# A decoder layer in float32: 16 of the weight sums of each down projection formed in the rounds before it

## The chip, the cores and the metric

The kernel runs on one core of a Trainium2 chip (trn2). The metric is the time of one execution on the device, in microseconds (us). The core has TensorE (PE, matmuls), VectorE (DVE), ScalarE (ACT), GpSimd (POOL) and SyncE (SP), which issues all the transfers between HBM and the on-chip memory; its queue is SPq in the rows.

## The reference, cut to what matters

```python
for i in range(DEPTH):                                  # DEPTH = 1, SEQ = 1024, D_MODEL = 1024, D_FF = 2816
    h = swiglu(rmsnorm(x, ffn1_pre_norm[i]), ffn1_w_gate[i], ffn1_w_up[i], ffn1_w_down[i])
    x = x + MACARON_WEIGHT * rmsnorm(h, ffn1_post_norm[i])
    h = hybrid_mixer(rmsnorm(x, mix_pre_norm[i]), ...)
    x = x + rmsnorm(h, mix_post_norm[i])
    h = swiglu(rmsnorm(x, ffn2_pre_norm[i]), ffn2_w_gate[i], ffn2_w_up[i], ffn2_w_down[i])
    x = x + MACARON_WEIGHT * rmsnorm(h, ffn2_post_norm[i])

def swiglu(x, w_gate, w_up, w_down):
    return (jax.nn.silu(x @ w_gate) * (x @ w_up)) @ w_down
```

The change touches the two feed-forward blocks (`f1` and `f2`) alone.

## The kernel before

**Precision and form.** Every float32 product is made of three matmuls in a faster format, from a high and a low part of each operand: hi x hi, hi x lo, lo x hi. ScalarE makes the high part (a cast), VectorE the low one (a subtraction). Large products are formed as seven smaller ones in place of eight, after Strassen's scheme; some of their operands are sums or differences of two blocks, which VectorE has to form first.

**The rounds.** A feed-forward block has 22 tiles of 128 hidden features. The first two are made plainly, the others in pairs: the loop variable `i` goes from 1 to 10, and each pair has the tiles `s = 0` and `s = 1`. `seven_pe` gives PE's order for one tile: seven products of 12 matmuls of 512 columns. `tile` in `ffn_dve` gives VectorE's: it takes the products out of PSUM, scales them, multiplies the up half by the gated half into `act_stage`, and in between forms the sums and low parts (`t3_sum`, `t2_sum`, `v1_low`, `t3_low` and so on) of the next tile. Where it does this differs by `s`: in tile `s = 0` `t3_sum` and `t2_sum` stand right after the third product's reads (L983, L985), ahead of the sum of L999; in tile `s = 1` they stand after L999 and L1001. PE's seventh product waits for L999 (`read(4)`), the first product of the next tile for `v1_low` (L895). SP loads the next tile's weights: `g_next` (gate, 512 KB, L410) waits until all seven low parts of the tile are formed, since the last of them, `g2_low` (L922), still reads the gate buffer; `v_next` (up, two loads of 256 KB, L413) waits for PE's products 1 and 4; `store` writes a tile's activations to HBM (L432). All of them stand in one queue in this order:

```python
                    g_next(i, 0)
                    v_next(i, 0, 0)
                    store(i - 1, 1)
                    v_next(i, 0, 1)
                    g_next(i, 1)
                    v_next(i, 1, 0)
                    store(i, 0)
                    v_next(i, 1, 1)
```

Before round 8 SP also issues the three loads of the first rows of activations for the down phase, 5.5 MB (`down_first_rows_sp`, L1308).

**The down phase** multiplies by the down weights: seven products `m = 0` to 6, each over `k = 0` to 10, four output parts `d`, 12 matmuls for a step `(m, k)`. The weight block of a step is a single block of the input (`m` = 2, 5) or a sum or difference of two: `DOWN_W` lists them. For these SP loads two blocks of 256 KB (`down_w_in`), VectorE adds them (`down_w_sum`, L1357), ScalarE casts (`down_w_hi`, L1372) and VectorE forms the low part (`down_w_lo`, L1388). The activations go the same way (`down_b_sum` L1363, `down_b_hi` L1383, `down_b_lo` L1395). Steps use 9 (f1) or 11 (f2) buffers in turn; the first ones are filled near the end of the rounds. The order of the down phase's steps on each engine isn't written by hand: `Plan.order` places them by costs and ranks given in `down_steps`, `first_turn_steps` and `end_plan`, together with what follows the block (the sums of squares, residuals and norms, and after f1 the first projections of the mixer).

Of the kernel before, what the change touches and what calls it, by code (L numbers as in the profile page):

```python
# [20 lines left out]
P = 128  # L21
# [59 lines left out]
    return (FG * m + k) % len(DOWN_SLOTS[p])  # L81


def w_loads(p, m, k):
    n = down_slot_of(p, m, k)
    return sum(min(len(DOWN_W[a]), 2) for a in range(m + 1) for b in range(FG)
               if (a, b) <= (m, k) and down_slot_of(p, a, b) == n)


W_SUMS = FG * sum(len(u) > 1 for u in DOWN_W)  # L90
B_SUMS = FG * sum(len(u) > 1 for u in DOWN_B)
FFN_COUNTS = {"gu_in0": 16, "gu_in1": 16, "gu_hi": PLAIN, "gu_lo": PLAIN, "gu_mm": 2 * PLAIN, "gate": 2 * PLAIN,
              "up": 2 * PLAIN, "silu": 2 * PLAIN, "prod": 2 * PLAIN, "s_act": 12, "s_dve": 21, "g_in": 16 * SEVEN,
# [3 lines left out]
              "dn_b_sum": B_SUMS, "dn_w_hi": FG * DOWN_N, "dn_b_hi": FG * DOWN_N, "dn_w_lo": FG * DOWN_N,  # L97
              "dn_b_lo": FG * DOWN_N, "dn_step": (FG - 1) * DOWN_N, "dn_mm": 4 * DOWN_N, "dn_put": len(PUTS),
              "dn_sum": len(SUMS), "dn_w_in9": 0, "dn_w_in10": 0}
for _n in range(9):  # L100
    FFN_COUNTS[f"dn_w_in{_n}"] = 16 * max(w_loads("f1", a, b) for a in range(DOWN_N) for b in range(FG)
                                          if down_slot_of("f1", a, b) == _n)
SHARED = {"dn_w_in0": ("turn_hi", KT), "dn_w_in1": ("turn_lo", KT), "dn_w_in2": ("turn_sq", KT), "dn_w_in3": ("turn_sum", KT - 1),
          "dn_w_in4": ("first_w_in", 16), "dn_w_in5": ("cols_in", 32), "dn_w_in6": ("consts_in", 64),
          "dn_w_in7": ("half_cols", 1), "dn_w_in8": ("first_w_hi", 1), "dn_b_first": ("first_w_lo", 1),
          "dn_b_second0": ("rope_sin", 2), "dn_w_in9": ("sd_x_mm", CH), "dn_w_in10": ("sd_cb_mm", CH)}
JOINT = {n: f"{old}_{new}" for new, (old, _) in SHARED.items() for n in (old, "ff_" + new)}


def build(nc, a):  # L110
    with ExitStack() as ctx:  # L111
        sems = {}

        def sem(name):
            if name[:3] in ("f1_", "f2_"):
                name = "ff_" + name[3:]
            name = JOINT.get(name, name)
            if name not in sems:
                sems[name] = ctx.enter_context(nc.semaphore(name))
            return sems[name]  # L120
# [6 lines left out]
        def wait(eng, name, value):  # L127

            if not isinstance(value, int) or value > 0:

                eng.wait_ge(sem(name), value + (FFN_COUNTS[name[3:]] if name[:3] == "f2_" else 0)
                            + (SHARED[name[3:]][1] if name[3:] in SHARED and name[0] == "f" else 0))


        nh = at("norm_hi", 0, [P, KT, S], FR)
# [121 lines left out]
        dsum = {p: at("down_sums_" + p, kb, [P, KT, S]) for p, kb in DOWN_SUMS.items()}  # L257
        res3 = at("residual_closing", 0, [P, KT, S])
        late = at("late_tokens", 64, [P, KT, S])
        dw_hi, dw_two, dw_lo, dw_raw, db_hi, db_lo, db_raw = ({} for _ in range(7))  # L260
        for p, slots in DOWN_SLOTS.items():
            dw_hi[p] = [at(f"{p}_down_w_hi_{n}", w, [P, 4, P], FR) for n, (w, _) in enumerate(slots)]
# [11 lines left out]


        acts = nc.dram_tensor("act_scratch", (FT, P, S), F32).ap()
        x1 = nc.dram_tensor("x1_scratch", (KT, P, S), F32).ap()
        x2 = nc.dram_tensor("x2_scratch", (KT, P, S), F32).ap()
        zscr = nc.dram_tensor("z_scratch", (Z_T, P, S), F32).ap()
# [141 lines left out]
        def ffn_sp(sp, p, wgu):  # L421
            def g_next(i, s):
                wait(sp, p + "_t_lo", at_tile(i, s, 7, 7))
                g_in_sp(sp, p, pair_of(wgu, i, s + 1))

            def v_next(i, s, n):
                wait(sp, p + "_seven", at_tile(i, s, 7, 4 if n else 1))
                v_in_sp(sp, p, pair_of(wgu, i, s + 1), n)

            def store(i, s):  # L430
                wait(sp, p + "_read", at_tile(i, s, 11, 11))
                sp.dma_start(pair_of(acts, i, s), stage[p][0][:]).then_inc(sem(p + "_act_out"), 16)  # L432
# [12 lines left out]
            def rounds(first, last):
                with sp.Fori(first, last) as i:
                    g_next(i, 0)
                    v_next(i, 0, 0)
                    store(i - 1, 1)
                    v_next(i, 0, 1)  # L450
                    g_next(i, 1)
                    v_next(i, 1, 0)
                    store(i, 0)
                    v_next(i, 1, 1)
            rounds(2, FIRST_ROWS)
            down_first_rows_sp(sp, p)
            rounds(FIRST_ROWS, LAST_PAIR)
            g_next(LAST_PAIR, 0)
            v_next(LAST_PAIR, 0, 0)
            store(LAST_PAIR - 1, 1)  # L460
            v_next(LAST_PAIR, 0, 1)
            down_start_sp(sp, p, store)


# [323 lines left out]
        def ffn_dve(v, p, t, pre):  # L788
# [181 lines left out]
                    else:  # L970
                        turn_half_dve(v, step, e, cols[:, 24:32], cols[:, pre:pre + KT])

            def tile(i, s, more):
                def product(n):
                    wait(v, p + "_seven", at_tile(i, s, 7, n))

# [22 lines left out]
                v.tensor_tensor(e4[:], banks(3), e4[:], ALU.add).then_inc(sem(p + "_read"), 1)  # L999
                had(4)  # L1000
                v.tensor_tensor(e4[:], e4[:], rb[:, half(0)], ALU.mult).then_inc(sem(p + "_read"), 1)  # L1001
                if s and more:
                    t3_sum(i, s + 1)
                    t2_sum(i, s + 1)
# [39 lines left out]
            tile(1, 0, True)  # L1044
            tile(1, 1, True)
            with v.Fori(2, LAST_PAIR) as i:
                tile(i, 0, True)
                tile(i, 1, True)
            tile(LAST_PAIR, 0, True)
            tile(LAST_PAIR, 1, False)  # L1050
            yield
# [12 lines left out]
        def down_steps(plan, p):  # L1064
# [8 lines left out]
            for m in range(DOWN_N):  # L1073
                for k in range(FG):
                    n = FG * m + k
                    ready = []
                    if n >= EARLY:
                        free = ("mm", *divmod(n - slots, FG)) if n >= slots else None
                        if n >= slots:
                            add("SP", "dw_in", ("dw_in", m, k), 6.0, free)  # L1080
                            if (m, k) == (1, 3):
                                add("SP", "dw_in", ("late_in",), 4.0)
                            elif (m, k) == (1, 6):
                                add("SP", "dw_in", ("b_in",), 4.0)
                        w = ("dw_in", m, k) if n >= slots else ("db_lo", m, k - 1) if k > EARLY else None
                        if len(DOWN_W[m]) > 1:
                            add("DVE", "w_sum", ("dw_sum", m, k), 0.61, w)
                            w = ("dw_sum", m, k)
                        add("ACT", "w", ("dw_hi", m, k), 0.54, w)
                        add("DVE", "w", ("dw_lo", m, k), 0.61, ("dw_hi", m, k))  # L1090
                        b = free
                        if len(DOWN_B[m]) > 1:
                            add("DVE", "b_sum", ("db_sum", m, k), 0.61, free)
                            b = ("db_sum", m, k)
                        add("ACT", "b", ("db_hi", m, k), 0.54, b)
                        add("DVE", "b", ("db_lo", m, k), 0.61, ("db_hi", m, k))
                        ready = [("dw_lo", m, k), ("db_lo", m, k)]
                    if k == 0 and m > 1:
                        ready += [u for d in range(4) for u in put_in(m - 2, d)]
                    if k == 0 and m == last:  # L1100
                        ready.append(end)
                    add("PE", "main", ("mm", m, k), 2.04 if p == "f2" and m == last else 2.72, *ready)
                if p == "f2" and m == last:
                    add("PE", "main", ("last",), 7.5)
                for d in range(4):
                    done = ("last",) if p == "f2" and (m, d) == (last, 3) else ("mm", m, FG - 1)
                    users = put_in(m, d)
                    for u in users:
                        engine = "ACT" if u[0] == "put" else "DVE"
                        before = [w for n in range(m) for w in put_in(n, d) if w[2:] == u[2:]]  # L1110
                        other = {(1, "add"): users[0], (4, "put"): users[-1]}.get((m, u[0]))
                        add(engine, u[0], u, 0.69, done, before[-1] if before else None, other)
# [140 lines left out]
        RSTD_RANK = {(x, "rstd"): 0 for x in ("PE", "ACT", "DVE")}  # L1253

        def w_sums(m, k):
            return FG * sum(len(x) > 1 for x in DOWN_W[:m]) + k + 1

        def b_sums(m, k):
            return FG * sum(len(x) > 1 for x in DOWN_B[:m]) + k + 1
# [39 lines left out]
        def down_w_in(sp, p, m, k):  # L1299
            down_slot(sp, p, m, k)  # L1300
            j = down_slot_of(p, m, k)
            for n, (out, rows) in enumerate(DOWN_W[m][:2]):
                to = dw_two[p][j] if n else dw_raw[p][j]
                sp.dma_start(to[:], a["d" + p[1]][FG * rows + k][:, 4 * out:4 * out + 4]).then_inc(sem(f"{p}_dn_w_in{j}"), 16)
# [60 lines left out]

        def down_w_hi(act, p, m, k):
            j = down_slot_of(p, m, k)
            if len(DOWN_W[m]) > 1:
                wait(act, p + "_dn_w_sum", w_sums(m, k))
            else:  # L1370
                down_w_loaded(act, p, m, k)
# [1912 lines left out]
```

## Time and profile before

| | us |
|---|---|
| median of 3 runs | 2229.76 (2228.91 to 2235.98) |
| the profiled execution, whole | 2235.22 |
| its span, first to last instruction | 2233.4 |
| PE busy | 2175.1 |
| DVE busy | 1748.0 |
| ACT busy | 1012.1 |

The mean granted clock of TensorE is 0.992. Rounds of block f1 run from about 65 to 450 us, its down phase to 666; the mixer to about 1560; rounds of f2 from about 1620 to 2000, its down phase to 2220. In a timeline row the first number is the start, the second the time of the instruction (or of x n of them in a row), and the brackets tell how long the engine was idle before it and what ended that.

### The profile page before, as it was taken

To read this page: it belongs to the slowest core of one execution; us is meant where nothing else is said; L and a number is where in the kernel's file an instruction comes from. 1 tells how busy PE (TensorE), PEld (TensorE's weight loads), DVE (VectorE), ACT (ScalarE), POOL (GpSimd) and SP (SyncE) were. 2 spreads that over 40 slices of the span, in tenths; PEclk is the share of its full clock that TensorE was granted. 3 is DMA by queue.
4 is the path that set the end of the run, shared out by engine and by line. 5 is a ranking of instruction groups with operands and counts; after the bars stand their busy time and mean duration, and the time that the engine had idled before them with its cause. 6 is when DMAs were issued, how large, how long until landed. Compare 5 with 4: busy or idle time off the path is not lost. (4 is left out here: it accounts for less than half of the span.)

```text
span 2233.4 us, 29464 instructions
## 1 busy us (share of the span) xinstructions
PE 2175.1 (97%) x10148; PEld 1778.8 (80%) x10148; DVE 1748.0 (78%) x2707; ACT 1012.1 (45%) x1837; POOL 229.5 (10%) x213
## 2 busy tenths in 40 slices
PE   9999999999998999999999999999999999999998
PEld 7788887878877877778788777788888888887887
DVE  8777777799898787786666676878877777779988
ACT  6323332255553576787632684323522322335454
POOL 0000000000000344444200233300000000000000
PEclk9999999999999999999999999999999999999999
DMA  4222234385453001001131124223132224247644
GB/s 145 66 85 85 85 119 154 95 310 176 164 192 102 29 10 38 31 18 58 42 102 48 64 107 172 83 79 120 66 95 85 83 83 170 83 154 269 224 139 160
DMA packets 101608, 245.00 MB, mean 110 GB/s; under 512 B 10752, under 2 KB 12800, under 8 KB 99968
## 3 DMA queue, kind: packets, MB, share of 16 engines
q1 hardware_dynamic: 101504, 243.65, 32.5%
q8 instruction: 60, 0.98, 0.2%
q14 instruction: 44, 0.36, 0.1%
HBM read 199.24 MB, written 44.37 MB: 109 GB/s over the span
## 5 line engine op out<-in xcount | busy, mean ns | idle before, releaser
L1399 PE MATMUL psum<-f_down_b_hi,f_down_w_hi 128*128 128x512 f32 x616 | 241.2, 392 | 6.2 <-DVE f_down_w_lo L1388 3.8
L1400 PE MATMUL psum<-f_down_b_lo,f_down_w_hi 128*128 128x512 f32 x616 | 240.4, 390 | 0.0
L1401 PE MATMUL psum<-f_down_b_hi,f_down_w_lo 128*128 128x512 f32 x616 | 240.4, 390 | 0.0
L690 ACT CAST plain_hi<-up_raw 128x512 fp32r<-128x512 f32 x80 | 49.5, 619 | 244.6 <-DMA up_raw<-in_gu 238.5
L716 ACT ACTIVATE sum<-sum 128x512 f32<-128x512 f32 x80 | 50.6, 633 | 212.0 <-DVE sum L1001 128.5
L1399 PEld LDWEIGHTS psum<-f_down_b_hi,f_down_w_hi 128*128 128x128 f32 x616 | 116.0, 188 | 33.7 <-DVE f_down_w_lo L1388 5.9
L694 ACT CAST t_hi<-t_raw 128x512 fp32r<-128x512 f32 x160 | 97.2, 620 | 87.2 <-DVE t_raw L890 81.6
L1401 PEld LDWEIGHTS psum<-f_down_b_hi,f_down_w_lo 128*128 128x128 f32 x616 | 116.0, 188 | 24.5
L1400 PEld LDWEIGHTS psum<-f_down_b_lo,f_down_w_hi 128*128 128x128 f32 x616 | 115.9, 188 | 23.9
L467 PE MATMUL psum<-norm_hi,plain_hi 128*128 128x512 f32 x320 | 125.5, 392 | 7.8 <-DVE up_lo L895 5.2
L2208 PE MATMUL psum<-norm_hi,tile_hi 128*128 128x512 f32 x320 | 129.1, 403 | 1.8 <-DVE z_scaled L2630 1.8
L2537 DVE TENSOR_TENSOR probs_t_lo<-psum,probs_t_hi 128x512 fp32r<-128x512 f32 x144 | 97.1, 685 | 39.3 <-ACT probs_t_hi L2452 38.4
L468 PE MATMUL psum<-norm_lo,plain_hi 128*128 128x512 f32 x320 | 125.2, 391 | 0.0
L469 PE MATMUL psum<-norm_hi,up_lo 128*128 128x512 f32 x320 | 125.1, 391 | 0.0
L2210 PE MATMUL psum<-norm_hi,tile_lo 128*128 128x512 f32 x320 | 124.9, 390 | 0.0
L2209 PE MATMUL psum<-norm_lo,tile_hi 128*128 128x512 f32 x320 | 124.8, 390 | 0.0
L467 PE MATMUL psum<-norm_hi,t_hi 128*128 128x512 f32 x320 | 124.5, 389 | 0.0
L468 PE MATMUL psum<-norm_lo,t_hi 128*128 128x512 f32 x320 | 124.5, 389 | 0.0
L467 PE MATMUL psum<-s_hi,t_hi 128*128 128x512 f32 x320 | 124.5, 389 | 0.0
L468 PE MATMUL psum<-s_lo,t_hi 128*128 128x512 f32 x320 | 124.5, 389 | 0.0
L469 PE MATMUL psum<-s_hi,t_lo 128*128 128x512 f32 x320 | 124.5, 389 | 0.0
L469 PE MATMUL psum<-norm_hi,t_lo 128*128 128x512 f32 x320 | 124.5, 389 | 0.0
(398 smaller groups left out, 5768.8 us busy)
## 6 DMA issues: line engine op xcount, KB each, us to landing
f_down_w_raw<-in_d SPq DMA_DIRECT2D x154, 256.0 KB, 2.8
f_down_w_two<-in_d SPq DMA_DIRECT2D x110, 256.0 KB, 3.8
act_scratch<-act_stage_f SPq DMA_DIRECT2D x44, 512.0 KB, 5.4
gate_raw<-in_gu SPq DMA_DIRECT2D x40, 512.0 KB, 4.4
up_raw<-in_gu SPq DMA_DIRECT2D x80, 256.0 KB, 4.4
raw_tile<-in_w_att SPq DMA_DIRECT2D x28, 512.0 KB, 3.5
act_first_rows<-act_scratch SPq DMA_DIRECT2D x4, 2048.0 KB, 11.1
act_second_rows<-act_scratch SPq DMA_DIRECT2D x8, 1024.0 KB, 8.7
```

Source lines behind the costliest of these rows:

```text
L467: pe.matmul(o, w_hi[:, k, :], a_hi(k), start=(k == 0 and not more), stop=False, skip_group_check=more)
L468: pe.matmul(o, w_hi[:, k, :], a_lo(k), start=False, stop=False, skip_group_check=more)
L469: mm = pe.matmul(o, w_lo[:, k, :], a_hi(k), start=False, stop=(k == KH - 1), skip_group_check=more)
L694: act.copy(to, of).then_inc(sem(p + "_t_hi"), 1)
L716: act.activation(x[:], x[:], ACT.Silu).then_inc(sem(p + "_s_out"), 1)
L1399: pe.matmul(o, dw_hi[p][j][:, d, :], db_hi[p][j][:], start=(k == 0), stop=False)
L1400: pe.matmul(o, dw_hi[p][j][:, d, :], db_lo[p][j][:], start=False, stop=False)
L1401: return pe.matmul(o, dw_lo[p][j][:, d, :], db_hi[p][j][:], start=False, stop=(k == FG - 1))
L2208: pe.matmul(banks(bank), wh[:, w % 2, k, :], nh[:, k, x], start=(k == 0), stop=False)
L2209: pe.matmul(banks(bank), wh[:, w % 2, k, :], nl[:, k, x], start=False, stop=False)
L2210: mm = pe.matmul(banks(bank), wl[:, w % 2, k, :], nh[:, k, x], start=False, stop=(k == KT - 1))
L2537: v.tensor_tensor(ptl[:, n % 2].rearrange("p a d -> p (a d)"), banks(4 + n % 2), pth[:, n % 2].rearrange("p a d -> p (a d)").bitcast(F32), ...
```

## The change

In `m` = 0 and `m` = 6 (`ROUND_SUMS`) the weight sums of the steps `k` = 3 to 10 are no longer formed in the down phase. In rounds `i` = 2 to 9 of the block, tile `s` loads the two blocks of one such step (`kept_in`: step `k = i + 1` of `m` = 0 for `s` = 0, of `m` = 6 for `s` = 1) into two fixed buffers of 2 KB per partition, VectorE adds them (`kept_add`, after L1001), and SP stores the sum to a new HBM tensor (`kept_store`). The down phase loads such a block with one transfer in place of two and has no VectorE sum for it: `summed` takes the step out of the plan too, so the planner orders the steps anew. `kept_in` waits for the store before it (`kept_out`), `kept_store` for the sum, the down phase's first weight load for all stores. Semaphores are shared with ones that exist.

```diff
+ROUND_SUMS = (0, DOWN_N - 1)
+ROUND_FIRST = 3
+ROUNDS = FG - ROUND_FIRST
+
+def kept_sum(m, k):
+    return m in ROUND_SUMS and k >= ROUND_FIRST
+
+def summed(m, k):
+    return len(DOWN_W[m]) > 1 and not kept_sum(m, k)
...
+        kept_raw = at("kept_weights", 160, [P, 4, P])
+        kept_two = at("kept_weights_two", 162, [P, 4, P])
...
+        kept = nc.dram_tensor("kept_weight_sums", (len(ROUND_SUMS) * ROUNDS, P, 4, P), F32).ap()
...
+            def kept_in(i, s):
+                wait(sp, p + "_kept_out", 16 * (2 * (i - 2) + s))
+                for n, (out, rows) in enumerate(DOWN_W[ROUND_SUMS[s]][:2]):
+                    w = a["d" + p[1]][FG * rows + ROUND_FIRST:FG * (rows + 1)]
+                    sp.dma_start((kept_two if n else kept_raw)[:], tile_of(w, i - 2)[:, 4 * out:4 * out + 4])\
+                      .then_inc(sem(p + "_kept_in"), 16)
+
+            def kept_store(i, s):
+                wait(sp, p + "_kept_sum", 2 * (i - 2) + s + 1)
+                sp.dma_start(tile_of(kept[ROUNDS * s:ROUNDS * s + ROUNDS], i - 2), kept_raw[:]).then_inc(sem(p + "_kept_out"), 16)
+
             def rounds(first, last):
                 with sp.Fori(first, last) as i:
                     g_next(i, 0)
+                    kept_in(i, 0)
                     v_next(i, 0, 0)
                     store(i - 1, 1)
                     v_next(i, 0, 1)
+                    kept_store(i, 0)
                     g_next(i, 1)
+                    kept_in(i, 1)
                     v_next(i, 1, 0)
                     store(i, 0)
                     v_next(i, 1, 1)
+                    kept_store(i, 1)
+            wait(sp, p + "_act_out", 16 * 2)
             rounds(2, FIRST_ROWS)
             down_first_rows_sp(sp, p)
             rounds(FIRST_ROWS, LAST_PAIR)
...
+            def kept_add(i, s):
+                wait(v, p + "_kept_in", 32 * (2 * (i - 2) + s + 1))
+                v.tensor_tensor(kept_raw[:], kept_raw[:], kept_two[:], DOWN_W[ROUND_SUMS[s]][2])\
+                 .then_inc(sem(p + "_kept_sum"), 1)
...
                 v.tensor_tensor(e4[:], e4[:], rb[:, half(0)], ALU.mult).then_inc(sem(p + "_read"), 1)
+                if keep:
+                    kept_add(i, s)
                 if s and more:
                     t3_sum(i, s + 1)
...
             with v.Fori(2, LAST_PAIR) as i:
-                tile(i, 0, True)
-                tile(i, 1, True)
+                tile(i, 0, True, True)
+                tile(i, 1, True, True)
...
-                        if len(DOWN_W[m]) > 1:
+                        if summed(m, k):
                             add("DVE", "w_sum", ("dw_sum", m, k), 0.61, w)
                             w = ("dw_sum", m, k)
...
         def down_w_in(sp, p, m, k):
             down_slot(sp, p, m, k)
             j = down_slot_of(p, m, k)
+            if kept_sum(m, k):
+                sp.dma_start(dw_raw[p][j][:], kept[ROUNDS * ROUND_SUMS.index(m) + k - ROUND_FIRST])\
+                  .then_inc(sem(f"{p}_dn_w_in{j}"), 16)
+                return
...
         def down_start_sp(sp, p, store):
             slots = len(DOWN_SLOTS[p])
             middle = slots - 4
+            wait(sp, p + "_kept_out", 16 * 2 * ROUNDS)
             down_w_in(sp, p, 0, 0)
...
-            if len(DOWN_W[m]) > 1:
+            if summed(m, k):
                 wait(act, p + "_dn_w_sum", w_sums(m, k))
```

The rest of the diff counts the loads and sums anew for the semaphores.

## Rows read from the trace of the kernel before

**Rows 1.** The page, busy us, share of the span, instructions of each engine.

```profile
PE 2175.1 (97%) x10148; PEld 1778.8 (80%) x10148; DVE 1748.0 (78%) x2707; ACT 1012.1 (45%) x1837; POOL 229.5 (10%) x213
```

**Rows 2.** PE's waits: waiter, releaser, us in total, times, longest.

```profile
PE psum L1399 <- DVE f_down_w_lo L1388: 3.8, 4, 1.9
PE psum L467 <- DVE sum L999: 3.1, 3, 1.7
```

**Rows 3.** Stretches: length, busy us of PE, PEld, DVE, ACT, POOL, clock, DMA.

```profile
200.00:250.00 50.00, 50.00 (x222) 41.40 (x221) 36.79 (x58) 14.39 (x26) 0.00 (x0) 1.00 0.26 81
449.60:480.00 30.40, 29.10 (x126) 23.16 (x125) 30.36 (x52) 15.74 (x29) 0.00 (x0) 1.00 0.95 341
```

**Rows 4.** Timeline of a tile s = 1 in f1: VectorE, then SP.

```profile
215.73 0.69 DVE L1001 TENSOR_TENSOR sum<-sum,rstd_rows 128x512 f32<-128x512 f32 x1
216.34 0.69 DVE L873 TENSOR_TENSOR t_raw<-gate_raw 128x512 f32<-128x512 f32 x1
...
226.69 0.69 DVE L922 TENSOR_TENSOR gate_lo<-gate_raw,plain_hi 128x512 fp32r<-128x512 f32 x1
...
227.55 0.33 SPq L410 DMA_DIRECT2D gate_raw<-in_gu  x1
```

**Rows 5.** Timeline of the tile s = 0 after it: VectorE, ScalarE, PE's seventh product.

```profile
232.06 0.69 DVE L873 TENSOR_TENSOR t_raw<-gate_raw 128x512 f32<-128x512 f32 x1 [1.94 <-DMA gate_raw<-in_gu]
232.98 0.69 DVE L879 TENSOR_TENSOR t_raw<-t_raw,up_raw 128x512 f32<-128x512 f32 x1 [0.22 <-DMA up_raw<-in_gu]
...
235.52 0.68 DVE L999 TENSOR_TENSOR sum<-psum,sum 128x512 f32<-128x512 f32 x1
...
232.88 0.63 ACT L690 CAST plain_hi<-up_raw 128x512 fp32r<-128x512 f32 x1 [6.25 <-DMA up_raw<-in_gu]
...
236.47 0.39 PE L467 MATMUL psum<-s_hi_a,plain_hi 128*128 128x512 f32 x1
```

**Rows 6.** L999 and PE's seventh product in a round of f2.

```profile
1711.62 0.68 DVE L999 TENSOR_TENSOR sum<-psum,sum 128x512 f32<-128x512 f32 x1
...
1712.92 0.39 PE L467 MATMUL psum<-s_hi_a,plain_hi 128*128 128x512 f32 x1
```

**Rows 7.** Timeline around the row loads before round 8 of f1.

```profile
330.01 0.69 DVE L1001 TENSOR_TENSOR sum<-sum,rstd_rows 128x512 f32<-128x512 f32 x1
...
328.26 1.50 SPq L1308 DMA_DIRECT2D act_first_rows<-act_scratch  x3
...
351.88 0.68 DVE L999 TENSOR_TENSOR sum<-psum,sum 128x512 f32<-128x512 f32 x1
...
352.61 0.50 PE L467 MATMUL psum<-s_hi_a,plain_hi 128*128 128x512 f32 x1 [1.69 <-DVE sum L999]
```

**Rows 8.** Weight loads of a quiet stretch of the down phase, us from issue to landing.

```profile
f_down_w_raw<-in_d SPq DMA_DIRECT2D x10, 256.0 KB, 2.7
f_down_w_two<-in_d SPq DMA_DIRECT2D x8, 256.0 KB, 3.0
```

**Rows 9.** Start of the down phases: PE's holes, and a stretch behind the second.

```profile
460.64 0.50 PE L1399 MATMUL psum<-f_down_b_hi,f_down_w_hi 128*128 128x512 f32 x1 [0.70 <-DVE f_down_w_lo L1388]
...
2013.92 0.50 PE L1399 MATMUL psum<-f_down_b_hi,f_down_w_hi 128*128 128x512 f32 x1 [1.91 <-DVE f_down_w_lo L1388]
...
2014.00:2020.00 6.00, 6.00 (x20) 4.76 (x21) 6.00 (x11) 3.65 (x6) 0.00 (x0) 0.72 1.05 400
```

**Rows 10.** End of block f1: a stretch, PE's holes, ScalarE's cast.

```profile
660.00:690.00 30.00, 24.95 (x109) 20.17 (x108) 23.37 (x34) 12.08 (x17) 0.00 (x0) 0.89 0.63 168
...
636.07 0.47 PE L1399 MATMUL psum<-f_down_b_hi,f_down_w_hi 128*128 128x512 f32 x1 [1.67 <-ACT rstd_rows L1531]
...
675.93 0.47 PE L2229 MATMUL psum<-norm_hi,first_q_hi_lo 128*128 128x512 f32 x1 [2.86 <-DVE norm_lo L1602]
...
673.33 1.04 ACT L2411 CAST tile_hi<-raw_tile 128x1024 fp32r<-128x1024 f32 x1 [5.60 <-DMA raw_tile<-in_w_att]
```

**Rows 11.** VectorE behind the last matmuls of f2.

```profile
2220.01 0.69 DVE L1454 TENSOR_TENSOR down_sums_f<-down_sums_f,psum 128x512 f32<-128x512 f32 x1 [3.06 <-PE psum L1401]
```

More of the change, by code:

```diff
@@ L81, in down_slot_of @@
     return (FG * m + k) % len(DOWN_SLOTS[p])
+ROUND_SUMS = (0, DOWN_N - 1)
[5 more added lines that the diff above has]
+    return len(DOWN_W[m]) > 1 and not kept_sum(m, k)
 def w_loads(p, m, k):
     n = down_slot_of(p, m, k)
-    return sum(min(len(DOWN_W[a]), 2) for a in range(m + 1) for b in range(FG)
+    return sum(2 if summed(a, b) else 1 for a in range(m + 1) for b in range(FG)
                if (a, b) <= (m, k) and down_slot_of(p, a, b) == n)
-W_SUMS = FG * sum(len(u) > 1 for u in DOWN_W)
+W_SUMS = sum(summed(a, b) for a in range(DOWN_N) for b in range(FG))
 B_SUMS = FG * sum(len(u) > 1 for u in DOWN_B)
@@ L99 @@
               "dn_sum": len(SUMS), "dn_w_in9": 0, "dn_w_in10": 0}
+KEPT = {"dn_w_in0": ("kept_in", 16 * 4 * ROUNDS), "dn_w_sum": ("kept_sum", 2 * ROUNDS),
+        "dn_b_second0": ("kept_out", 16 * 2 * ROUNDS)}
 for _n in range(9):
@@ L106 @@
           "dn_b_second0": ("rope_sin", 2), "dn_w_in9": ("sd_x_mm", CH), "dn_w_in10": ("sd_cb_mm", CH)}
+KEPT_OF = {kept: (new, count) for new, (kept, count) in KEPT.items()}
+for _n, (_, _count) in KEPT.items():
+    FFN_COUNTS[_n] += _count
 JOINT = {n: f"{old}_{new}" for new, (old, _) in SHARED.items() for n in (old, "ff_" + new)}
@@ L115, in sem @@
             if name[:3] in ("f1_", "f2_"):
-                name = "ff_" + name[3:]
+                name = "ff_" + KEPT_OF.get(name[3:], (name[3:],))[0]
             name = JOINT.get(name, name)
@@ L129, in wait, with offset @@
             if not isinstance(value, int) or value > 0:
-                eng.wait_ge(sem(name), value + (FFN_COUNTS[name[3:]] if name[:3] == "f2_" else 0)
-                            + (SHARED[name[3:]][1] if name[3:] in SHARED and name[0] == "f" else 0))
+                eng.wait_ge(sem(name), value + offset(name))
+        def offset(name):
+            p, rest = name[:3], name[3:]
+            if p not in ("f1_", "f2_"):
+                return 0
+            after = KEPT[rest][1] if rest in KEPT else 0
+            rest = KEPT_OF.get(rest, (rest,))[0]
+            return after + (FFN_COUNTS[rest] if p == "f2_" else 0) + (SHARED[rest][1] if rest in SHARED else 0)
         nh = at("norm_hi", 0, [P, KT, S], FR)
@@ L971, in ffn_dve, with tile @@
                         turn_half_dve(v, step, e, cols[:, 24:32], cols[:, pre:pre + KT])
-            def tile(i, s, more):
+            def kept_add(i, s):
+                wait(v, p + "_kept_in", 32 * (2 * (i - 2) + s + 1))
+                v.tensor_tensor(kept_raw[:], kept_raw[:], kept_two[:], DOWN_W[ROUND_SUMS[s]][2])\
+                 .then_inc(sem(p + "_kept_sum"), 1)
+            def tile(i, s, more, keep=False):
                 def product(n):
@@ L1255, in w_sums @@
         def w_sums(m, k):
-            return FG * sum(len(x) > 1 for x in DOWN_W[:m]) + k + 1
+            return sum(summed(x, y) for x in range(m + 1) for y in range(FG) if (x, y) <= (m, k))
         def b_sums(m, k):
```

## The prediction, made before the changed kernel ran

> **What bounds the kernel now.** I read four views in this order. The page's engine table shows TensorE (PE) busy for 2175 of the 2233 us, VectorE (DVE) for 1748 [rows 1]: the time is PE's work plus some 58 us of holes, so an edit to VectorE's work counts only where PE waits for it. The list of PE's waits says where: in the down phases (matmuls of L1399) only 3.8 us for the low weight parts of VectorE, and in the rounds 3.1 us, three times, for the sum of L999 [rows 2]. Then the stretches: one of the rounds has PE at 50.00 of 50 us with VectorE at 36.8, but at the start of the down phase VectorE is full [rows 3]. So 16 VectorE instructions are taken out of full stretches and put into stretches where a quarter of the engine is idle. On shares alone that is a gain. The timeline of one round says what the shares hide.
>
> **A round has two tiles; call them A (s = 0) and B (s = 1).** In a tile B, VectorE takes L999 and L1001 (215.73) right behind the fifth product and then runs without a gap to `gate_lo` (L922, 226.69 to 227.38). Only then is `g_raw` free: SP issues the gate load at 227.55, and the first up load and the store behind it [rows 4]. In tile A VectorE sits idle 1.94 us for the gate load (until 232.06) and 0.22 us more for the up load (232.98); then come t2, `v1_low`, `t3_low`, L993 and L999 in its fixed order, L999 at 235.52. PE's seventh product of A needs L999: it ends at 236.20, and the product starts at 236.47 [rows 5]. From a case where PE did wait (L999 from 351.88 for 0.68, PE at 352.61, [rows 7]) the signal takes 0.05 us. The slack is 236.47 - 236.25 = 0.22 us. So the loop "VectorE's end of B, load, VectorE in A" takes all but 0.2 us of PE's time for two tiles. In a round of the second block it is 1712.92 - 1712.35 = 0.57 us [rows 6]; between the two I take 0.3 for that block.
>
> **What the change adds in a round.** (1) One VectorE sum per tile, behind L1001. Consecutive independent sums start 0.61 us apart (215.73 to 216.34 [rows 4]), so B's sum puts `gate_lo` and the gate load 0.6 us later against PE. A's own sum comes after L999, and B waits for PE three times before it needs anything of it: nothing. B's sum also comes before `v1_low`, for which PE's next tile waits; if PE stalls there, it's a part of the same 0.6 and not added. (2) Two loads of 256 KB stand on SP right behind the gate load and ahead of the first up load. Their waits are met (the store they wait for was issued half a tile before). The up load lands later by their transfer. In the down phase the pair of such loads, issued 0.37 us apart, lands after 2.7 and 3.0 us: 0.67 us each, 1.35 for two; behind the gate load, 256 KB took 0.82 us (232.06 to ScalarE's cast at 232.88), 1.64 for two [rows 5, 8]. SP's issue (0.37 us apart above) isn't the bound, the transfer is. I take 1.5, between two near rows; the ends stay for the range. Tile B takes its gate and up data only after L1001, when all has landed: nothing. (3) One store per tile, off the path except in one round. (4) One wait per tile on SP for VectorE's sum, with the later gate load queued behind it; that load is due 9 us later.
>
> The Trainium skill ("DMA: Bandwidth & Descriptors", Queues, rings and completion order) states that each DMA engine takes the descriptors of one issuing queue in ring order, by which the pair's data does come ahead of the up load; the landings above are in the order of issue. Another section of that page (Anatomy of one DMA, for transfers issued by GpSimd) gives some 2 us fixed plus the bytes at 436 GB/s for each transfer; laid end to end that would make the pair an estimated 5.2 us, and a round's stall near 5.6 us in place of 1.9. The row speaks against adding it up: two loads issued 0.37 us apart landed 0.7 us apart [rows 8].
>
> **Sum of the rounds.** Ordinary round, block one: 0.6 + 1.5 - 0.2 = 1.9 us; block two, slack 0.3: 1.8. The kept sums run in rounds i = 2 to 9. Round 2 has no sum in the B before it (1.3 and 1.2); tile A of the last pair (i = 10) has no pair of loads but follows a B with a sum (0.4 and 0.3). Six ordinary rounds (3 to 7 and 9): 11.4 and 10.8. Round 8 is apart: before it SP issues the three loads of `act_first_rows` (L1308), which fill the queue; today that makes the gate come late and PE wait 1.69 us. With the change SP must first wait for B's sum in round 7: L1001 starts at 330.01, the sum at 330.62, it ends near 331.3, the store is issued, and the row loads go out near 331.9, not at 328.26 [rows 7]. The full queue ends 3.6 us later and the pair's 1.5 come on top: 5.1 us more. That makes a hole of near 7 us. A hole of 1.91 us was followed by 6 us with a mean granted clock of 0.72, a part of it at the lower level (1.2 of 2.4 GHz), so by 0.28 x 6 = 1.7 us of lost work [rows 9]; 5.1 + 1.7 = 6.8. The second block's round 8 is built alike: 6.8. Rounds: 1.3 + 11.4 + 6.8 + 0.4 = 19.9 and 1.2 + 10.8 + 6.8 + 0.3 = 19.1, together +39 us.
>
> **What it removes.** Sixteen sums a block, each 0.6, but only as holes of PE. At the down phase's start PE waits at k = 3 for 0.70 and 1.91 us [rows 9]. The planner gives the step a sum first; its cast waits for that, and the casts and low parts of the activations, which wait for nothing, are set ahead of it. With nothing to sum, the cast and `w_lo` of k = 3 can stand first. I take both holes and the clock's 1.7 as gone: -4.3. Near the end of block one the hole of 1.67 us ends with ScalarE's row copy, which stands behind a square that waits for VectorE's adds: -0.8, half of it. Behind it lie 5.05 us of idle PE in 660 to 690 and a clock of 0.89, 3.3 us: 8.4 in all [rows 10]. But the longest hole (2.86 us) ends through ScalarE, which sits on `tile_hi` until a raw tile has landed at 673.33; eight sums fewer (4.8 us) help only if the new order puts `norm_hi` first. Bounds 0 and 8.4, I take 4. The kernel's end waits for PE (3.06 us idle before the last add [rows 11]): 0. The halved loads at the down start meet no wait of PE but the one counted. Together -9.
>
> **Result.** +39 - 9 = +30 us. Profiled execution: 2235.2 (span 2233.4) to 2265. It lies 5.5 us over the median 2229.76 of the three runs; the step is put on the median: **2260 us**.
>
> **Rivals.**
> *The pair of loads costs the up load nothing* (its data overtakes, or mixes into gaps). Then a round pays 0.6 less the slack, 0.35, and round 8 pays 3.6 + 1.7: 12 x 0.35 + 0.6 + 10.6 - 9 = +6, 2236. For it: landing is mostly latency (4.4 us for a gate). Against: queue order. 0.12.
> *The clock falls in ordinary rounds too.* The new holes have 1.5 to 1.9 us; of today's, 1.69 and 1.67 were not followed by a fall, 1.91 was [rows 7, 9, 10]. If half of twelve rounds lose 1.7: +10, and up to +20: 2270 to 2280. 0.20.
> *Faster: the rounds take all of it.* One mechanism: L999 of tile A doesn't become later than PE's seventh product, because the pair lands in the 1.94 us in which VectorE waits for the gate anyway and up data comes with it. It decides at 0.22 us of added lateness. Then only the -9 stays (-13 if the tail gives all): 2221, down to 2216. Against: PE already waited where the loads came late [rows 2, 7]. 0.07.
> *It doesn't do what it says*, or the new order of the down phases loses: the counts add up (8 rounds, 2 sums), so only the order is open; some us either way. 0.04.
> Forecast as summed: 0.57.
>
> **Range and chances.** Low end of the forecast: 1.35 for the pair and a slack of 0.57 give 1.4 a round; with 13 to 15 us of gains +13, 2243. High end: 1.64, little gain and a few clock falls, 2280. To take in most of the first rival and of the clock's: 2238 to 2284. A measurement of this kernel tells some 0.3% (7 us) from no change: faster 0.07, same 0.07, slower 0.86.
>
> **What would show it.** PE's wait for L999 grows from 3 times to some 16, near 35 us in all, longest near 7 in round 8 of each block; in tile A VectorE's idle time moves from the gate load to the up load (0.22 to some 1.7); the gate loads of tile B's end issue near 40 us apart, not 38; the holes at k = 3 are gone. It would be wrong if `up_raw` lands as early after the gate load as now, or if PE runs the rounds without holes.

## The result and the profile after

| | before | after |
|---|---|---|
| median | 2232.28 (2228.91 to 2235.98, 4 runs) | 2271.19 (2265.82 to 2272.89, 4 runs) |
| span of the profiled execution | 2233.4 | 2270.8 |
| mean granted clock | 0.992 | 0.989 |

The ratio is 1.0174, 95% interval 1.0153 to 1.0195: some 39 us slower. The forecast was 2260, slower. One of the four executions of e2 below took 2710.8 us at a mean granted clock of 0.75 and is left out of its median. Lines have moved: L999 is now L1048, L1001 L1050, L873 and L879 L917 and L923, L410 and L413 L438 and L441, L1308 L1363, L467 L511, L1399 L1455. The sum that was added is L1019, the loads L477, the store L482.

The page's engine table, and PE's waits (waiter, releaser, us in total, times, longest), answer to [rows 1, 2]:

```profile
PE 2186.0 (96%) x10148; PEld 1781.0 (78%) x10148; DVE 1749.6 (77%) x2707; ACT 1012.4 (45%) x1837; POOL 228.7 (10%) x213
```

```profile
PE psum L511 <- DVE sum L1048: 33.3, 16, 4.6
...
PE psum L1455 <- DVE f_down_w_lo L1444: 1.2, 2, 0.6
```

VectorE does the same 2707 instructions. PE's wait for its sum went from 3 times to 16, the waits for `w_lo` in the down phase from 4 to 2: the change traded two short holes for sixteen.

The timeline of one round of f1 answers to [rows 4, 5]: VectorE in tile B, SP, VectorE in tile A, PE's seventh product.

```profile
225.58 0.69 DVE L1050 TENSOR_TENSOR sum<-sum,rstd_rows 128x512 f32<-128x512 f32 x1
226.19 0.68 DVE L1019 TENSOR_TENSOR kept_weights<-kept_weights,kept_weights_two 128x512 f32<-128x512 f32 x1
...
238.01 0.33 SPq L438 DMA_DIRECT2D gate_raw<-in_gu  x1
238.66 0.33 SPq L477 DMA_DIRECT2D kept_weights<-in_d  x1
239.18 0.33 SPq L477 DMA_DIRECT2D kept_weights_two<-in_d  x1
239.78 0.33 SPq L441 DMA_DIRECT2D up_raw<-in_gu  x1
...
242.81 0.69 DVE L917 TENSOR_TENSOR t_raw<-gate_raw 128x512 f32<-128x512 f32 x1 [2.44 <-DMA gate_raw<-in_gu]
...
245.67 0.69 DVE L923 TENSOR_TENSOR t_raw<-t_raw,up_raw 128x512 f32<-128x512 f32 x1 [2.17 <-DMA up_raw<-in_gu]
...
248.95 0.50 PE L511 MATMUL psum<-s_hi_a,plain_hi 128*128 128x512 f32 x1 [2.07 <-DVE sum L1048]
```

From L1050 to the gate load are 12.43 us (before, L1001 to the gate load, 11.82): the sum's 0.61. From the gate's first use to the up block's are 2.86 us where there were 0.92. Over the twelve ordinary rounds (3 to 7 and 9 of both blocks) the medians are 0.92 before and 2.78 after; from the gate's issue to its use 4.49 and 4.43, from the gate's issue to the up block's use 5.41 and 7.25. So the up data comes 1.8 us later. The loop that the prediction describes then takes 0.6 + 1.8 - 0.2 = 2.2 us more than PE's 38.08 for two tiles.

The same program in stretches (length, busy us of PE, PEld, DVE, ACT, POOL, granted clock, DMA share, GB/s), first before, then after: rounds of f1, its down phase, its end and the first projections, rounds of f2, down phase and end.

```profile
65.40:451.50 386.10, 383.57 (x1681) 316.29 (x1681) 283.52 (x441) 116.20 (x203) 0.00 (x0) 0.99 0.32 103
451.50:665.40 213.90, 211.54 (x931) 174.00 (x932) 197.71 (x321) 112.12 (x192) 0.00 (x0) 1.00 0.61 207
665.40:757.80 92.40, 85.56 (x447) 70.57 (x446) 72.70 (x125) 34.72 (x58) 11.67 (x11) 0.96 0.30 87
1620.00:2003.60 383.60, 381.81 (x1681) 315.02 (x1681) 283.71 (x441) 115.64 (x202) 0.00 (x0) 1.00 0.32 104
2003.60:2233.40 229.80, 221.81 (x1006) 183.36 (x1006) 208.56 (x339) 113.35 (x197) 0.00 (x0) 0.99 0.59 202
```

```profile
65.20:478.35 413.15, 394.45 (x1680) 320.21 (x1680) 292.42 (x457) 116.95 (x203) 0.00 (x0) 0.97 0.38 128
478.35:690.90 212.55, 210.96 (x931) 174.16 (x932) 193.88 (x312) 113.47 (x195) 0.00 (x0) 1.00 0.58 193
690.90:776.80 85.90, 81.53 (x446) 68.81 (x445) 67.80 (x118) 32.60 (x55) 11.27 (x11) 1.00 0.26 80
1636.40:2045.70 409.30, 391.92 (x1681) 318.38 (x1681) 292.62 (x457) 116.28 (x202) 0.00 (x0) 0.98 0.38 127
2045.70:2270.80 225.10, 219.73 (x1006) 182.45 (x1006) 199.13 (x323) 112.48 (x197) 0.00 (x0) 1.00 0.55 189
```

The rounds take 27.05 and 25.7 us more, +52.7 together. All the rest takes 1448.4 us (span less the rounds) where it took 1463.7: -15.3. Part of the 52.7 is PE that waits (33.3 us listed against 3.1); part is PE that is busy for longer with the same matmuls (+10.9 and +10.1), most of it by the clock: 0.97 and 0.98.

Round 8 answers to [rows 7]: the timeline with VectorE's sum, the row loads, gate, VectorE in tile A and PE, and then the stretch behind the hole.

```profile
349.30 0.69 DVE L1019 TENSOR_TENSOR kept_weights<-kept_weights,kept_weights_two 128x512 f32<-128x512 f32 x1
350.15 0.35 SPq L482 DMA_DIRECT2D kept_weight_sums<-kept_weights  x1
350.77 1.56 SPq L1363 DMA_DIRECT2D act_first_rows<-act_scratch  x3
...
369.31 0.69 DVE L917 TENSOR_TENSOR t_raw<-gate_raw 128x512 f32<-128x512 f32 x1 [5.83 <-DMA gate_raw<-in_gu]
371.29 0.69 DVE L923 TENSOR_TENSOR t_raw<-t_raw,up_raw 128x512 f32<-128x512 f32 x1 [1.29 <-DMA up_raw<-in_gu]
...
374.56 0.80 PE L511 MATMUL psum<-s_hi_a,plain_hi 128*128 128x512 f32 x1 [4.58 <-DVE sum L1048]
```

```profile
374.00:384.00 10.00, 9.44 (x31) 7.57 (x32) 9.70 (x16) 4.02 (x7) 0.00 (x0) 0.72 0.07 26
```

The hole grew from 1.69 to 4.58, and the 10 us behind it have a clock of 0.72.

### The profile page after: what moved, and what is told of

It reads as the page before. It is cut to its first block, busy times and chain, and to the rows that moved or that the text cites. A ratio compares the mean times of both kernels' runs of the same rounds, so it can differ in the third digit from the quotient of the medians.

```text
span 2270.8 us, 29800 instructions
## 1 busy us (share of the span) xinstructions
PE 2186.0 (96%) x10148; PEld 1781.0 (78%) x10148; DVE 1749.6 (77%) x2707; ACT 1012.4 (45%) x1837; POOL 228.7 (10%) x213
## 4 chain that ended last, share of the span: by engine, by line
PE 69%; DVE 15%; issue 5%; DMA 5%; ACT 3%; SPq 1%; POOL 1%; DVEq 1%; ACTq 0%; POOLq 0%
PE psum L511 7%; PE psum L512 6%; PE psum L513 6%; PE psum L1455 6%; PE psum L1456 5%; PE psum L1457 5%; DMA up_raw<-in_gu 4%; PE psum L2264 3%; PE psum L2266 3%; PE psum L2265 3%; PE psum L2418 2%; PE psum L636 2%; PE psum L638 1%; PE psum L637 1%; PE psum L2821 1%
## 5 line engine op out<-in xcount | busy, mean ns | idle before, releaser
L1455 PE MATMUL psum<-f_down_b_hi,f_down_w_hi 128*128 128x512 f32 x616 | 240.3, 390 | 3.6 <-ACT rstd_rows L1587 2.4
L1455 PEld LDWEIGHTS psum<-f_down_b_hi,f_down_w_hi 128*128 128x128 f32 x616 | 115.6, 188 | 29.8 <-issue 4.0
L511 PE MATMUL psum<-norm_hi,plain_hi 128*128 128x512 f32 x320 | 128.6, 402 | 9.4 <-DVE up_lo L939 5.2
L511 PE MATMUL psum<-norm_hi,t_hi 128*128 128x512 f32 x320 | 124.7, 390 | 0.0
L511 PE MATMUL psum<-s_hi,t_hi 128*128 128x512 f32 x320 | 124.5, 389 | 0.0
```

The costliest lines, as they stand in the source:

```text
L511: pe.matmul(o, w_hi[:, k, :], a_hi(k), start=(k == 0 and not more), stop=False, skip_group_check=more)
L1455: pe.matmul(o, dw_hi[p][j][:, d, :], db_hi[p][j][:], start=(k == 0), stop=False)
```

## The experiments

"Rounds" in this table is the sum of the two stretches of the rounds in the profiled execution, "rest" its span less that. The ratio is to the kernel before in runs on the same chip, with its 95% interval.

| kernel | rounds | rest | median | ratio |
|---|---|---|---|---|
| before | 769.7 | 1463.7 | | 1 |
| after | 822.4 | 1448.4 | 2271.2 | 1.0174 [1.0153, 1.0195] |
| e1 pair behind the up load | 792.2 | 1452.3 | 2246.0 | 1.0074 [1.0056, 1.0093] |
| e2 sum of one column | 806.5 | 1448.3 | 2262.5 | 1.0148 [1.0128, 1.0168] |
| e3 a quarter of the bytes | 792.6 | 1450.5 | 2249.2 | 1.0085 [1.0068, 1.0102] |
| e4 row loads first | 826.7 | 1452.6 | 2271.3 | 1.0176 [1.0159, 1.0193] |
| e5 down phase alone | 774.2 | 1451.0 | 2221.0 | 0.9952 [0.9934, 0.9970] |
| e6 rounds alone | 818.6 | 1466.9 | 2279.2 | 1.0200 [1.0179, 1.0221] |
| e7 sum at the tile's start | 771.7 | 1451.7 | 2226.5 | 0.9973 [0.9957, 0.9990] |
| e8 = e1 + e2 | 782.9 | 1449.9 | 2237.6 | 1.0018 [1.0005, 1.0031] |
| e9 = e7 again | | | 2224.1 | 0.9968 [0.9956, 0.9980] |
| e10 = e5 again | | | 2223.9 | 0.9954 [0.9941, 0.9967] |

The profiled execution is one of several and not the median one: in e2 it lies 6 us below the median, in e5, e6 and e4 it lies 6, 8 and 10 us above. So the two middle columns tell differences of 10 us and more, and single waits, not a few us.

### e1 and e2: the pair's place, and the sum

e1 swaps two lines of SP, in both tiles:

```diff
                     g_next(i, 0)
-                    kept_in(i, 0)
                     v_next(i, 0, 0)
+                    kept_in(i, 0)
```

> The same work, only the pair of loads of the kept blocks is issued behind the first up load and not ahead of it. Theory (the up load comes late because the pair stands ahead of it in the queue, and VectorE's sum of L1048 with it): the wait of VectorE for the up load in a tile s = 0 goes back from some 2 us to some 0.2, an ordinary round costs 0.6 - 0.2 = 0.4 us and not 2.3, round 8 keeps most of its hole (its row loads are still issued late); 2271 falls to about 2234. Rival (the traffic itself, or VectorE's sums, wherever they stand): stays at 2262 or more.

e2 lets VectorE add one column of 512, the waits and transfers as they are:

```diff
-v.tensor_tensor(kept_raw[:], kept_raw[:], kept_two[:], DOWN_W[ROUND_SUMS[s]][2])
+v.tensor_tensor(kept_raw[:, 0, 0:1], kept_raw[:, 0, 0:1], kept_two[:, 0, 0:1], DOWN_W[ROUND_SUMS[s]][2])
```

> VectorE's sum in the rounds is done over one of its 512 columns (the others stay unsummed), everything else as in the changed kernel. Theory (of a round's 2.3 us the sum in tile s = 1 makes 0.6, the pair of loads the rest): 12 rounds x 0.6 and one or two clock falls fewer, 2271 falls to about 2260. Rival (VectorE's added instructions are the cost, the loads are hidden): the rounds cost nothing, about 2222.

By the medians e1 took 25 us off and e2 9, by the ratios 22 and 6: the pair's place is the larger part, the sum the smaller. The intervals of e2 and of the change overlap; what speaks for e2's gain is the distance between PE's seventh products of tile A, 40.0 us in the median of the ordinary rounds where the change has 40.7. And e1 stayed 12 us above what was expected. In its trace 5.84 us pass from the gate's issue to the use of the up block in the ordinary rounds (median; before 5.41, after 7.25), so a pair issued *behind* the up load still holds it up, by 0.4 us:

```profile
235.97 0.69 DVE L917 TENSOR_TENSOR t_raw<-gate_raw 128x512 f32<-128x512 f32 x1 [1.96 <-DMA gate_raw<-in_gu]
...
237.41 0.69 DVE L923 TENSOR_TENSOR t_raw<-t_raw,up_raw 128x512 f32<-128x512 f32 x1 [0.76 <-DMA up_raw<-in_gu]
...
240.69 0.50 PE L511 MATMUL psum<-s_hi_a,plain_hi 128*128 128x512 f32 x1 [0.17 <-DVE sum L1048]
...
361.32 0.79 PE L511 MATMUL psum<-s_hi_a,plain_hi 128*128 128x512 f32 x1 [3.35 <-DVE sum L1048]
```

The sum's 0.6 and this 0.4, less the slack of 0.2, are the ordinary round of e1 (median 39.0 us without round 9, where 38.08 was expected to become 38.5). Round 8 still has 3.35 us, and the interval behind it 40.87 us in both blocks, 2.7 more than before.

### e8: both

The edits of e1 and e2 together.

> The pair of loads stands behind the first up load (as in e1_pair_behind_up, 2246), and the sum is over one column of 512 (the kept blocks are wrong in the others, so this part of the sum is left out). e1 stayed 12 us over its forecast; its ordinary rounds take 38.8 to 39.4 us against 38.08 before, with PE waiting about 0.2 us for the seventh product in tile A and 0.3 for the third group of tile B, each with 0.1 to start again. If that is the sum's 0.6 us on VectorE, the rounds come to within 0.2 us of 38.08 and the time falls by 10 to 14: 2232 to 2236. Rival: it is the transfers beside the up load, and the time stays within 4 us of 2246.

8.4 us less than e1 by the medians, 0.56% or 12 us by the ratios, where 10 to 14 were expected. The ordinary rounds without round 9 fell from 39.0 to 38.27 us (medians), within the 0.2 of 38.08 that was expected, so e1's excess there was the sum. With the ratios of e1, e2, e8 and the change there is a square: moving the pair is worth 1.0% with the sum in place and 1.3% without it; the sum is worth 0.3% with the pair in front and 0.6% with it behind. The pair's place and the sum behind the moved pair are clear of the intervals; the 0.3% alone is not, nor is it shown that one weighs more once the other is gone. e8 is still 0.66% (15 us) above e5, whose rounds hold no kept work. A part of it is round 8, whose holes are 3.02 and 2.97 us in e8, 2.52 and 1.30 in e5; the rest was not taken apart.

### e3: bytes or number

The two loads stay ahead of the up load, but each brings 64 KB, not 256; the sum has its full length and reads that quarter again and again.

```diff
-sp.dma_start((kept_two if n else kept_raw)[:], tile_of(w, i - 2)[:, 4 * out:4 * out + 4])
+sp.dma_start((kept_two if n else kept_raw)[:, 0:1], tile_of(w, i - 2)[:, 4 * out:4 * out + 1])
```

> The two loads of a round's tile bring a quarter of their bytes (64 KB each), VectorE's sum keeps its full width of 512 columns (it reads the loaded quarter over again; most of the sum is left out). Theory (the up load is late by the pair's transfer): it comes 0.5 us later and not 1.9, a round costs 0.9 us and not 2.3, clock falls mostly gone: about 2246. Rival (each transfer costs a fixed time whatever its size): stays within 5 us of 2271.

22 us less than the change, 3 above the expected time. The rival, a fixed price for each load that makes most of the cost, has fallen. From the gate's issue to the use of the up block the medians of the ordinary rounds are 5.41 us before, 7.25 after, 5.96 here: 0.55 of 1.84 us stay with a quarter of the bytes. In the change and in e3 alike SP issues the up load 1.76 us behind the gate load, before 0.58 (medians). So the 1.3 us that are gone are the bytes'; whether the other 0.55 belong to the bytes that are left or to the later issue was not separated. The Trainium skill ("DMA: Bandwidth & Descriptors", Anatomy of one DMA) has some 2 us for each transfer regardless of size, for transfers issued by GpSimd; two loads issued by SP did not pay it one after the other.

### e4: the row loads of round 8 ahead of the store

```diff
-            rounds(2, FIRST_ROWS)
+            rounds(2, FIRST_ROWS - 1)
+            rounds(FIRST_ROWS - 1, FIRST_ROWS, False)
             down_first_rows_sp(sp, p)
+            kept_store(FIRST_ROWS - 1, 1)
```

`False` leaves out `kept_store(i, 1)`, which follows the row loads now.

> The same work, but the three row loads before round 8 are issued ahead of the kept store of round 7, so they no longer wait for VectorE's sum. Theory (the late row loads make a part of round 8's hole of 4.6 us): the hole falls to about 3 in each block, and the clock's fall behind it may go: 2271 falls by 4 to 8, about 2265. Rival (the pair alone makes that hole): no change, 2271.

No gain, and round 8's hole grew from 4.58 to 7.23 us. (Lines of e4 are three further down.) The row loads did leave 1.3 us earlier against VectorE's kept sum (0.17 behind its start, 1.47 in the change) and the gate's use came 0.9 us earlier against it, but the store now stood behind them, and the next pair waits for that store:

```profile
347.33 1.49 SPq L1366 DMA_DIRECT2D act_first_rows<-act_scratch  x3
348.86 1.42 SPq L482 DMA_DIRECT2D kept_weight_sums<-kept_weights  x1
358.98 0.35 SPq L438 DMA_DIRECT2D gate_raw<-in_gu  x1
...
365.06 0.34 SPq L477 DMA_DIRECT2D kept_weights<-in_d  x1
...
366.19 0.33 SPq L441 DMA_DIRECT2D up_raw<-in_gu  x1
...
366.22 0.69 DVE L920 TENSOR_TENSOR t_raw<-gate_raw 128x512 f32<-128x512 f32 x1 [4.89 <-DMA gate_raw<-in_gu]
...
371.80 0.69 DVE L926 TENSOR_TENSOR t_raw<-t_raw,up_raw 128x512 f32<-128x512 f32 x1 [4.89 <-DMA up_raw<-in_gu]
```

SP stood from 359 to 365 us in the wait of `kept_in`, with the up load queued behind it. So this is a new wait in place of the old one, and no verdict on the theory of the late row loads. What speaks for that theory is that the gate's use follows the issue of the row loads at a fixed distance wherever the gate load is issued 10 to 12 us behind them: 18.54 us after the change (350.77 to 369.31), 18.57 in e1, 18.89 here, and 18.3 to 18.9 in both blocks of these and of e2, e3, e6 and e8. Before, with the gate load issued 14 us behind them, it is 20.35 and 19.73. And in e7 (below), whose row loads leave ahead of VectorE's scaled sum as before, the holes of round 8 are 2.22 and 1.35 us, where e8 has 3.02 and 2.97.

### e5 and e6: the two halves apart

e5 takes the kept work out of the rounds and loads for each of the 16 steps one block of the input, unsummed:

```diff
-sp.dma_start(dw_raw[p][j][:], kept[ROUNDS * ROUND_SUMS.index(m) + k - ROUND_FIRST])
+sp.dma_start(dw_raw[p][j][:], a["d" + p[1]][FG * rows + k][:, 4 * out:4 * out + 4])
```

> The gains alone. The rounds are those of the kernel before (no loads, sums or stores in them); the 16 steps of each block's down phase load one weight block straight from the input, as after the change one from HBM. The 16 sums of each block are left out. If the balance of the two traces is right (rounds +52.7, other stretches -12.5), this takes about 12.5 us less than before: 2218 to 2221, with PE's holes of 0.70 and 1.91 at step k=3 gone. Rival: most of the 12.5 comes from the clock and not from the change, and the time is within 4 us of before (2228 to 2234).

e6 keeps all of the rounds and gives the down phases back their own loads and sums:

```diff
 def summed(m, k):
-    return len(DOWN_W[m]) > 1 and not kept_sum(m, k)
+    return len(DOWN_W[m]) > 1
```

> The cost alone. Loads, sums and stores stand in the rounds as in the change; the down phases load and add their two blocks as before and never read what was kept. If cost and gain add up, this takes about 12.5 us more than the change: 2280 to 2286, +50 over before, with the holes at k=3 back. Rival: the gain of the down phase hangs on the later start of it, and this takes as long as the change, 2271.

The gain alone is 0.48% (e10: 0.46%), 10 to 11 us, and the cost alone 2.00%, 45 us, each a little smaller than expected (12.5 and 50). They add up to 1.5%, against 1.74% for the change, within their intervals. PE's waits in e6 show both lists at once, the rounds of the change and the down phase of before:

```profile
PE psum L511 <- DVE sum L1048: 31.7, 16, 4.6
...
PE psum L1455 <- DVE f_down_w_lo L1444: 3.7, 4, 1.9
```

### e7, e9 and e10: the same work where VectorE is idle

Each kept sum moves from behind L1050 to the start of a tile, where VectorE waits for PE's third product. Its loads are issued behind the second up load of the tile before, its store behind the first up load:

```diff
                     g_next(i, 0)
-                    kept_in(i, 0)
                     v_next(i, 0, 0)
+                    kept_store(i, 0)
                     store(i - 1, 1)
                     v_next(i, 0, 1)
-                    kept_store(i, 0)
+                    kept_in(i, 1)
                     g_next(i, 1)
-                    kept_in(i, 1)
                     v_next(i, 1, 0)
+                    kept_store(i, 1)
                     store(i, 0)
                     v_next(i, 1, 1)
-                    kept_store(i, 1)
+                    kept_in(i + 1, 0)
...
+                if keep:
+                    kept_add(i, s)
                 product(3)
```

> All of the work is there, moved: each sum stands at the start of a tile, where VectorE is idle 1.1 to 1.3 us before its wait for PE's third product; its two loads are issued behind the second up load of the tile before, and its store behind the first up load. If the cost is made of the pair ahead of the up load and of the 0.6 us of the sum in the chain to PE's seventh product, both go, and the time is that of the down phase's gain: 2218 to 2224, with PE's waits for the sum near before's. Rival: the added transfers (0.75 MB a tile) slow gate and up load wherever they stand, and at least 10 us of the cost stay: 2232 or more.

> The kernel of e7_sum_at_start again, in more rounds and beside e10. Its trace shows the rounds of both blocks at 771.7 us against 769.7 before, and the rest of the program at 1451.7 against 1463.7, so 10 us less than before: 2221 to 2227, ratio 0.9955 to 0.998. Rival: its lead over before (0.27%, interval 0.04% to 0.43% off the edge of 1) was chance, and the ratio is 0.999 or more.

> The kernel of e5_down_alone again (the 16 sums left out, one unsummed block loaded in their place), beside e9 on the same chip. If the rounds of e9 bear loads, sums and stores at no cost, the two are within 2 us of each other, as their spans are (2223.4 and 2225.2). Rival: the 5.5 us between their medians are real, the price of the traffic, and e10 is 4 us or more below e9.

All of the work is in it, and it is faster than both kernels: 0.32% under before (interval 0.20 to 0.44% in e9) and 2.1% under the change. The interval of e7 alone is 0.10 to 0.43% under before (the recorded text of e9 has 0.04). e7's 2226.5 lay 2.5 us over the expected span; e9's 2224.1 lay in its own. The timeline of e9 shows the order, its stretch and PE's waits what it does (its lines are 13 to 15 further down: L1063 is L1048):

```profile
189.21 0.69 DVE L1032 TENSOR_TENSOR kept_weights<-kept_weights,kept_weights_two 128x512 f32<-128x512 f32 x1
189.47 0.33 SPq L438 DMA_DIRECT2D gate_raw<-in_gu  x1
...
190.63 0.69 DVE L1047 TENSOR_TENSOR sum<-psum,first_product 128x512 f32<-128x512 f32 x1 [0.73 <-PE psum L526]
...
194.01 0.69 DVE L930 TENSOR_TENSOR t_raw<-gate_raw 128x512 f32<-128x512 f32 x1 [1.96 <-DMA gate_raw<-in_gu]
194.74 0.69 DVE L936 TENSOR_TENSOR t_raw<-t_raw,up_raw 128x512 f32<-128x512 f32 x1
195.96 0.35 SPq L477 DMA_DIRECT2D kept_weights<-in_d  x1
```

```profile
190.00:240.00 50.00, 50.00 (x221) 41.12 (x220) 37.95 (x60) 14.92 (x26) 0.00 (x0) 1.00 0.45 142
```

```profile
PE psum L524 <- DVE sum L1063: 3.9, 2, 2.1
```

The kept sum (L1032) now comes behind `gate_lo`, so the gate load doesn't wait for it, and in front of L1047 VectorE still has 0.73 us to spare. PE is at 50.00 of 50 us, as in [rows 3], with 142 GB/s moving in place of 81. What is left over e5 is 0.2 us by the medians of e9 and e10 and 5.5 by those of e7 and e5; the intervals overlap, so whether the traffic costs up to 0.2% stays open.

## Why the prediction was right, point by point

Direction, mechanism and place were right; the total was 11 us low (the step 39 us and not 30). That it came so near owes something to luck: the clock and the ordinary rounds cost 14.5 us more than forecast, round 8 and the rest of the program 9.1 less. The table splits the +52.7 us of the rounds by the distance between PE's seventh products of neighbouring rounds, each against the same distance before.

| term | forecast | measured |
|---|---|---|
| ordinary rounds, 12 | 22.2 | 26.1 |
| round 2, two | 2.5 | 4.3 |
| round 8, two, without clock | 10.2 | 7.4 |
| last pair, two | 0.7 | 1.0 |
| clock | 3.4 | 14.0 |
| outside the rounds | -9 | -15.3 |

*B's sum, 0.6.* Right: 0.61. PE's stall ahead of B's first product was not added to it, as argued: ordinary rounds without a fall of the clock take 39.8 to 40.9 us, median 40.3, the 2.2 us more that the loop gives.

*The pair, 1.5.* Mis-sized: 1.8. That is above even the upper bound, 1.64 from [rows 5]. Twelve times 0.3 is most of the ordinary rounds' 3.9 us. The prediction took SP's issue of the pair from the down phase (0.37 us apart) and set it aside; in the rounds the pair puts the up load's issue 1.18 us later (1.76 behind the gate load, not 0.58), and e3 leaves open whether a part of the 1.8 is that.

*Round 8.* The row loads left 3.8 us later against VectorE (2.08 behind L1050, before 1.75 ahead of L1001), as forecast (3.6). The step that failed is the next one, that the gate would be as much later: it came 2.0 us later (20.62 from L1050, 18.60 before). So 1.8 us of the delay was taken up: before, the gate was used 20.35 us behind the row loads, longer than the 18.3 to 18.9 measured in the experiments above, so it was something else that set the time there. The pair added 1.25 there (gate to up 1.98, before 0.73). Hole: 4.58, not near 7.

*The clock.* The forecast counted a fall only in round 8. Five intervals between seventh products are 1.7 to 3.2 us over the 40.3 of their neighbours (43.53, 41.98 and 42.52 in f1, 42.24 and 42.23 in f2), 11 us in all, each behind a hole of PE (2.90, 2.07 and 4.58 in f1, 1.85 and 4.60 in f2). The rows of three of them:

```profile
120.00:130.00 10.00, 7.10 (x21) 5.37 (x20) 8.43 (x14) 4.05 (x7) 0.00 (x0) 0.68 0.22 86
246.00:256.00 10.00, 7.93 (x28) 6.03 (x28) 9.66 (x16) 3.64 (x7) 0.00 (x0) 0.83 0.11 43
1857.00:1867.00 10.00, 10.00 (x38) 8.06 (x37) 9.07 (x15) 4.02 (x7) 0.00 (x0) 0.83 0.07 26
```

Three more came at the start of f2's rounds; the traces don't show that they come from the change (last section). So the rival "the clock falls in ordinary rounds too" (2270 to 2280) described the result better than the forecast itself, though of the twelve ordinary rounds' holes only two were followed by a fall, and besides them that of round 2 in f1.

*The gains.* The holes at k = 3 are gone as argued (2 waits for `w_lo` in place of 4, 0.6 the longest). The end of block one, taken at 4 between 0 and 8.4, gave 6.5 in its stretch. The block's down phase ends at 690.9 us where it ended at 665.4, so 685.5 to 715.5 us answers to the stretch of [rows 10]; PE's 5.05 idle us are gone from it, and the clock is 1.00 in place of 0.89:

```profile
685.50:715.50 30.00, 30.00 (x158) 25.83 (x157) 21.76 (x32) 9.97 (x15) 0.00 (x0) 1.00 0.60 165
```

The hole at ScalarE's row copy, for which half of 1.67 us was counted, stayed (1.59). Of the -15.3 some 2.6 us lie between the two blocks' stretches (859.6 us for 862.2), where the last 80 us have a clock of 0.95 for 0.91; no edit reaches there. e5 and e10, with 10 to 11 us, give the measure of the gain: 1 to 2 above the forecast.

*The other rivals.* "The pair costs nothing" fell with e1: moving it gave 25 us. "Faster" fell in the same way: the seventh product of tile A did become late, 16 times. But its idea, that these 16 instructions can run for nothing in the rounds, is what e7 does, once they are placed for it.

## What to carry to other kernels

An engine that is idle for a quarter of a loop has its gaps in certain places. Before work is moved there, find the chain that comes back to the start of the loop (here: VectorE's end of a tile, a load, VectorE's start) and how much slack it has; an instruction inside the chain costs its full length less that slack, one in a gap costs nothing. The same holds for the queue that issues loads: where the sum, its loads and its store stand decided between 1.7% slower and 0.3% faster with the same work. And price a small hole of PE with the chance that the clock falls behind it.

## What the runs showed of the hardware that was not expected

A load issued behind another still delays it. In e1 and e8 the pair stood behind the up load. From the gate load's issue to the use of the up block 5.84 and 5.67 us passed (medians of the ordinary rounds), before 5.41; in e7, with the pair 5.9 us behind the up load's issue and not 0.65, it was 5.27. The gate itself was used earlier in e1 and e8 (4.10 and 3.99 us behind its issue, before 4.49); why is open. The Trainium skill ("DMA: Bandwidth & Descriptors", Two DMAs through the same engine are not ordered) says that descriptors of one queue start in order but are pipelined; the rows agree, and the prediction had used only the first half of that.

Whether the clock falls isn't decided by the hole alone. A hole of 2.64 us ahead of f2's rounds is in all twelve traces. Over the 8 us behind it the granted clock was 1.00 in six of them, 0.79 to 0.81 in five and 0.62 after the change; both traces of the kernel of e5 have a fall, both of e7's have none. Before and after:

```profile
1619.97 0.50 PE L467 MATMUL psum<-norm_hi,plain_hi 128*128 128x512 f32 x1 [2.64 <-DVE up_scaled L1860]
...
1620.00:1628.00 8.00, 8.00 (x35) 6.64 (x36) 6.49 (x9) 2.28 (x5) 0.00 (x0) 1.00 0.28 69
```

```profile
1636.38 0.79 PE L511 MATMUL psum<-norm_hi,plain_hi 128*128 128x512 f32 x1 [2.64 <-DVE up_scaled L1916]
...
1636.40:1644.40 8.00, 8.00 (x23) 6.30 (x24) 6.50 (x9) 2.29 (x5) 0.00 (x0) 0.62 0.25 71
```

That is 3.0 us (0.38 x 8), in the rounds' +52.7. Likewise a hole of 1.97 us (168.07) and one of 1.89 (1898.94) were not followed by a fall, one of 1.85 (1856.70) was.
